# A decoder step with 32 streamed experts: two set-aside blocks of 2 MB that are filled twice, picks by replaced maxima, and sample logits behind the first gather

## The reference, cut to what matters

```python
h = rms_norm(x, norm2_g) * (1.0 + sc2) + sh2
logits = h @ router_w + router_b                 # 264 x 32
top_val, top_idx = lax.top_k(logits, 4)
gate = jax.nn.softmax(top_val, axis=-1)
...
u = xblk @ w_up[e] + b_up[e]                     # 1024 x 2048 per expert, 8 MB
act = glu * jax.nn.sigmoid(1.702 * glu) * (lin + 1.0)
return act @ w_down[e] + b_down[e]               # 1024 x 1024 per expert, 4 MB
```

## Time and profile before

| | before |
|---|---|
| median of 3 runs | 1181.11 us (1179.96 to 1181.35) |
| the profiled execution's own time | 1180.3 us |
| its span, first to last instruction | 1178.5 us |
| PE busy | 1118.9 us, 95% of the span |
| DVE, ACT, POOL busy | 413.6, 191.0, 29.2 us |
| moved by DMA | 460.96 MB, mean 391 GB/s |

### The profile page before, as it was taken

One profiled execution on the slowest core, in us unless ns is written; L12 is line 12 of the kernel. 1 busy time (PEld: TensorE's weight loads), 2 busy tenths in 40 slices (PEclk: granted clock), 3 DMA queues, 4 the chain that ended last, 5 costly groups with the idle time before them and its releaser, 6 DMA issues.

```text
span 1178.5 us, 14278 instructions
## 1 busy us (share of the span) xinstructions
PE 1118.9 (95%) x5652; PEld 499.4 (42%) x5652; DVE 413.6 (35%) x847; ACT 191.0 (16%) x384; POOL 29.2 (2%) x59
## 2 busy tenths in 40 slices
PE   6999998999999999999999989999999999999996
PEld 4777676763333333333333333333333333333332
DVE  3135552352333333333333343333333333333324
ACT  2161222221111111111111111111111111111112
POOL 0201010000000000000000000000000000000001
PEclk8999999999999999999999999999999999999999
DMA  9998994879999999999999999999999999999995
GB/s 348 360 309 220 355 288 156 356 263 408 392 428 429 428 427 428 427 428 429 429 429 429 428 427 427 429 428 426 428 428 427 429 427 428 428 430 427 427 428 207
DMA packets 51178, 460.96 MB, mean 391 GB/s; under 512 B 7012, under 2 KB 7984, under 8 KB 24472
## 3 DMA queue, kind: packets, MB, share of 16 engines
q1 hardware_dynamic: 44864, 449.66, 92.3%
q0 software_dynamic: 2752, 9.47, 3.3%
q10 hardware_dynamic: 3512, 1.14, 0.4%
HBM read 455.60 MB, written 4.65 MB: 391 GB/s over the span
## 4 chain that ended last, share of the span: by engine, by line
PE 64%; DMA 26%; DVE 1%; ACT 1%; issue 0%; ACTq 0%; DVEq 0%; SPq 0%
PE bank L1408 25%; DMA ring<-in_w_up 23%; PE bank L1462 13%; PE bank L1058 5%; PE bank L1449 5%; PE bank L1379 3%; DMA ring<-in_w_down 3%; PE bank L1293 3%; PE bank L1426 2%; PE bank L1022 1%; PE bank L1388 1%; PE bank L1178 1%; PE bank L1437 1%; PE bank L1155 1%; PE bank L1259 1%
## 5 line engine op out<-in xcount | busy, mean ns | idle before, releaser
L1408 PE MATMUL bank<-ring,arena 128*64 128x512 f32 x2032 | 452.6, 595 | 26.4 <-DMA ring<-in_w_up 25.0
L1408 PEld LDWEIGHTS bank<-ring,arena 128*64 128x64 f32 x2032 | 141.4, 137 | 328.1 <-issue 276.9
L1462 PE MATMUL bank<-ring,arena 128*64 128x512 f32 x1024 | 227.2, 595 | 1.6 <-DMA ring<-in_w_down 1.6
L1462 PEld LDWEIGHTS bank<-ring,arena 128*64 128x64 f32 x1024 | 70.8, 137 | 135.7 <-issue 132.8
L1058 PE MATMUL bank<-arena,ring 128*128 128x264 f32 x448 | 109.2, 399 | 2.7 <-DMA ring<-in_w_in 1.9
L1058 PEld LDWEIGHTS bank<-arena,ring 128*128 128x128 f32 x448 | 85.2, 195 | 20.6 <-issue 3.8
L2022 DVE COPY arena<-bank 128x512 f32<-128x512 f32 x32 | 22.1, 691 | 204.2 <-PE bank L1408 204.2
L881 ACT ACTIVATE arena<-bank 128x512 f32<-128x512 f32 x32 | 19.1, 598 | 445.7 <-PE bank L1408 445.7
L2076 DVE TENSOR_TENSOR arena<-bank,arena 128x512 f32<-128x512 f32 x32 | 22.1, 691 | 189.4 <-PE bank L1462 189.4
L1449 PE MATMUL bank<-arena 64*128 64x512 f32 x256 | 80.7, 627 | 0.8 <-issue 0.8
L2071 DVE TENSOR_TENSOR arena<-arena,bank 128x512 f32<-128x512 f32 x128 | 79.1, 680 | 5.4 <-PE bank L1449 5.4
(11 more groups left out here) (327 smaller groups left out, 679.8 us busy)
## 6 DMA issues: line engine op xcount, KB each, us to landing
ring<-in_w_up SPq DMA_DIRECT2D x126, 2048.0 KB, 31.2
ring<-in_w_down SPq DMA_DIRECT2D x63, 2048.0 KB, 29.0
ring<-in_w_ada SPq DMA_DIRECT2D x16, 1024.0 KB, 14.7
ring<-in_w_in SPq DMA_DIRECT2D x14, 1024.0 KB, 15.7
ring<-in_w_ada SPq DMA_DIRECT2D x16, 512.0 KB, 11.3
ring<-in_w_o SPq DMA_DIRECT2D x4, 1024.0 KB, 14.1
ring<-in_state_hgrn POOLq DMA_DIRECT2D x4, 512.0 KB, 14.4
arena<-sample_values POOLq DMA_DIRECT2D x4, 512.0 KB, 14.4
```

What stands on the lines that cost most here:

```text
L1408: last = mm(bank[64 * half:64 * half + 64, b, :], xe[:, par, k % 4, k // 4, :], src[:, 512 * half:512 * half + 512], start=(k == 0), stop= ...
L1462: last = mm(bank[64 * half:64 * half + 64, b, :], acts[:, k, :], pairs[:, slot, D * kk + 512 * half:D * kk + 512 * half + 512], start=(k = ...
```

## The change

Four things change.

**A second set-aside block, and both are filled twice.** A tile `more` of 128 x 3 x 1024 and 1024 columns of `arena` make a second block of 2 MB. Loads 8 and 9 go to the two blocks, and so do loads 18 and 19. Three of the four pieces of load 9 are issued behind the last load of the front, ahead of load 0; the fourth comes after loads 6 and 7, once the prompt's logits are made. The first load into a used ring slot is now load 10 (`FIRST_REFILL`). By the new `load_ahead`, loads 10 to 27 each wait for the load ten before them, and load 28 waits for 20, load 29 for 21, and so on (eight apart), as before the change.

**Picks by replaced maxima.** The logits get four more columns with a huge value, so that the eight maxima are these four and the four best. `match_replace` puts another value in place of all eight, and `picked` is where the logits and the result differ. The gates are computed on all 32 experts and masked by `picked`.

**Order in the routing stretch.** The dummy matmuls go. The count matmuls and the samples' logits and blocks come behind the first gather. All row vectors come behind the first `turn`. The new value of `x` for the prompt is signalled before that for the samples, and ACT squares the samples apart.

**Space.** The constructor's scratch for software-made descriptors is set to 4096 bytes for each partition, where it was left at its default. Some small tiles move or go. The unrolled rounds at the start are 4 instead of 3, and the round with the biases is 16 instead of 15.

```diff
-ASIDE = UPS + UP_FIRST + DOWNS
+ASIDE_AT = UPS + UP_FIRST + DOWNS
+FIRST_REFILL = ASIDE_AT + 2
+ASIDES = (ASIDE_AT, ASIDE_AT + 1, FIRST_REFILL + PAIRS, FIRST_REFILL + PAIRS + 1)
 def ring_place(i):
-    return i - (i > ASIDE)
+    return i - sum(i > a for a in ASIDES)
 def load_ahead(i):
     r = ring_place(i) - PAIRS
-    return r + (r >= ASIDE)
+    return next(j for j in range(r, r + len(ASIDES) + 1) if j not in ASIDES and ring_place(j) == r)
...
+        more = sb("more", [P, 3, 1024])
+        gpickT = sb("gpickT", [P, TP])[:, :]
...
-        aside = [[r_gv[:, 0:1024], r_gv[:, 2112:3136]], [r_qf[:, 2048:3072], r_s[:, 512:1536]]]
+        aside = [[r_gv[:, 0:1024], r_gv[:, 2112:3136], r_qf[:, 2048:3072], r_s[:, 512:1536]],
+                 [more[:, 0, :], more[:, 1, :], more[:, 2, :], r_gv[:, 1024:2048]]]
...
                     if i == UPS + UP_FIRST:
-                        load_aside()
-                    if i == ASIDE:
+                        sp.wait_ge(sem("on_ready"), 4)
+                        sp.wait_ge(sem("S2_out"), 48)
+                        load_aside(ASIDES[0])
+                    if i == ASIDES[0]:
+                        sp.wait_ge(sem("logit_psum"), 1)
+                        load_aside(ASIDES[1], (3,))
+                    if i in ASIDES[:2]:
+                        continue
+                    if i in ASIDES:
+                        name, value = expert_released(ASIDES[ASIDES.index(i) - 2], 0)
+                        sp.wait_ge(sem(name), value)
+                        load_aside(i)
                         continue
                     reuse(i, q)
...
+            load_aside(ASIDES[1], (0, 1, 2))
             for i in range(UPS):
                 reuse(i)
                 load(i, 0, "up", i)
...
-            keep_going(7)
             pe.wait_ge(sem("picked_ready"), 1)
             for i in range(2):
                 for j in range(i + 1):
-                    mm(bank[:, 2, P + NE * i:P + NE * i + NE], before[:, :] if j == i else ones[:, :], picked[:, j, :],
-                       start=(j == 0), stop=(j == i))
-            for j in range(2):
-                last = mm(bank[:, 2, P + 3 * NE:P + 4 * NE], ones[:, :], picked[:, j, :], start=(j == 0), stop=(j == 1))
+                    last = mm(bank[:, 2, P + NE * i:P + NE * i + NE], before[:, :] if j == i else ones[:, :], picked[:, j, :],
+                              start=(j == 0), stop=(j == i))
             last.then_inc(sem("rank_psum"), 1)
...
                 for i in tiles:
-                    od.did(v.max_index(top_i[:, i, :], top_v[:, i, :], logit[:, i, :]))
+                    od.did(v.match_replace(replaced[:, i, :], top_v[:, i, :], logit[:, i, :], -ABOVE))
                 od.settle()
                 own = slice(tiles[0], tiles[-1] + 1)
-                od.link(v.tensor_copy(top_f[:, own, :], top_i[:, own, 0:TOPK]))
-                for i in tiles:
-                    od.did(TT(onehot[:, i], iota_exp[:, :].unsqueeze(1).to_broadcast([P, TOPK, NE]),
-                              top_f[:, i, :].unsqueeze(2).to_broadcast([P, TOPK, NE]), ALU.is_equal))
-                od.settle()
+                od.link(TT(picked[:, own, :], logit[:, own, 0:NE], replaced[:, own, 0:NE], ALU.not_equal), sem("picked_ready"))
...
-    nc = bacc.Bacc("TRN2", target_bir_lowering=False, num_devices=1)
+    nc = bacc.Bacc("TRN2", target_bir_lowering=False, num_devices=1, dynamic_dma_scratch_size=4096)
```

More of the change, by code:

```diff
@@ L19 @@
 I32 = mybir.dt.int32
-U32 = mybir.dt.uint32
 U8 = mybir.dt.uint8
@@ L45 @@
 LIMIT = 7.0
+ABOVE = 3.0e38
 NQ = 6
@@ L841, in _ @@
                 act.wait_ge(sem("x1_ready"), k + 1)
-                od.did(A(tmpT[:, k, :], xT[:, k, :], ACT.Square), sem("sq_ready"))
+                od.did(A(tmpT[:, k, 0:TP], xT[:, k, 0:TP], ACT.Square), sem("sq_ready"))
+                if k == KT - 1:
+                    act.wait_ge(sem("x1s_ready"), KT)
+                    od.did(A(tmpT[:, :, TP:T], xT[:, :, TP:T], ACT.Square), sem("sq_ready"))
                 if k == 0:
@@ L902, in _ @@
             act.wait_ge(sem("gate_sub"), 1)
-            od.did(A(gate[:, :, :], gate[:, :, :], ACT.Exp), sem("gate_exp"))
+            od.did(A(gateE[:, :, :], gateE[:, :, :], ACT.Exp), sem("gate_exp"))
             for i in range(2):
@@ L1356, in _, with samples_routed @@
                 for j in range(i + 1):
-                    mm(bank[:, 2, P + NE * i:P + NE * i + NE], before[:, :] if j == i else ones[:, :], picked[:, j, :],
-                       start=(j == 0), stop=(j == i))
-            for j in range(2):
-                last = mm(bank[:, 2, P + 3 * NE:P + 4 * NE], ones[:, :], picked[:, j, :], start=(j == 0), stop=(j == 1))
+                    last = mm(bank[:, 2, P + NE * i:P + NE * i + NE], before[:, :] if j == i else ones[:, :], picked[:, j, :],
+                              start=(j == 0), stop=(j == i))
             last.then_inc(sem("rank_psum"), 1)
-            pe.wait_ge(sem("h2s_ready"), 1)
-            for k in range(KT):
-                last = mm(bank[0:TS, 3, 0:NE], h2T[:, k, TP:T], wrt[:, k, :], start=(k == 0), stop=(k == KT - 1))
-            last.then_inc(sem("logit_psum"), 1)
-            spread_d(3 * P, TS, lambda g: h2T[:, g:KT:2, TP:T]).then_inc(sem("xs_psum"), 1)
+            def samples_routed():
+                pe.wait_ge(sem("h2s_ready"), 1)
+                spread_d(3 * P, TS, lambda g: h2T[:, g:KT:2, TP:T]).then_inc(sem("xs_psum"), 1)
+                for k in range(KT):
+                    mm(bank[0:TS, 3, 0:NE], h2T[:, k, TP:T], wrt[:, k, :], start=(k == 0), stop=(k == KT - 1))
+                for j in range(2):
+                    last = mm(bank[:, 3, NE:2 * NE], ones[:, :], picked[:, j, :], start=(j == 0), stop=(j == 1))
+                last.then_inc(sem("logit_psum"), 1)
             def gather(n, first_blocks=True):
@@ L1389, in turn, with up @@
                 last.then_inc(sem("turned"), 1)
-            def up(par, k0, k1, loads, rounds, first=False, parts=False):
+            def up(par, k0, k1, loads, rounds, first=False, parts=None):
                 for s in range(k0, k1):
                     slot = loads(s)
-                    if slot is None:
-                        pe.wait_ge(sem("aside_in"), 64)
+                    if slot < 0:
+                        pe.wait_ge(sem("aside_in"), rounds(s))
                     else:
                         pe.wait_ge(sem(f"pair{slot}"), rounds(s))
-                    if parts and s == UPS - 1:
+                    if s == parts:
                         pe.wait_ge(sem("parts_in"), 32)
@@ L1579, in _ @@
             total = LOADS * NE
-            full = [16 * sum(expert_slot(m) == expert_slot(OVER_FIRST + i) for m in range(total) if m != ASIDE) for i in range(LOADS)]
+            full = [16 * sum(expert_slot(m) == expert_slot(OVER_FIRST + i) for m in range(total) if m not in ASIDES) for i in range(LOADS)]
             pe.wait_ge(sem("table_ready"), 1)
```

123 lines of the change are left out of this document (59 added, 64 removed).

## The result

| | before | changed kernel |
|---|---|---|
| median, all runs on this chip | 1179.84 us (1176.37 to 1181.35, 6 runs) | 1171.74 us (1170.14 to 1175.94, 6 runs) |
| the profiled execution's own time | 1180.3 us | 1170.1 us |
| its span | 1178.5 us | 1168.4 us |

The ratio is 0.9936, 95% interval 0.9915 to 0.9957: faster by 5.1 to 10.0 us. The forecast was 1176.6, in a range of 1174.6 to 1178.9.

The account below looks back on a forecast made before the run. DMA was taken as the bound: its last standstill, plus remaining loads at 4.90 us each, plus a fixed tail. Median 1181.1 less 4.5 (ring 4.4, routing 0.1) gave 1176.6 us, range 1174.6 to 1178.9.

Parts of the forecast that it names:

- the base of the sum: Starting figures of the kernel before: span 1178.5 us and median 1181.1, from which 4.4 and 0.1 us of gains were subtracted.
- rival 1: PE, without dummies, drops to half clock around 248 us; costs some 1.7 us, load 30 at 1178.3's pace; chance 0.08.
- The ring: Second filling closes DMA's hole at load 18; load 30 becomes the last dry place, landing at 365.7 not 370.1: 4.4 us gained.
- The pieces: Loads 18 and 19 as eight 512 KB pieces move at 401 GB/s against 430: 0.7 us, hidden, so nothing paid.
- slack: At load 30: the stream could land it at 364.0, PE's release allows 365.7, so 1.7 us of DMA delay costs nothing.
- The second block: Its 2 MB load into DMA holes at 177 and 250 us: no cost, and no gain with only one filling.
- The routing stretch: Picks to first expert matmul: gather starts near 246.2, then 5.6 us of PE work, `up` at 251.8: 0.1 us gained.
- Rival 3: POOL's state transfers wait because the 4096-byte scratch is too small; 1184.6 us if the fourth is 8 us late; chance 0.05.
- the cover: POOL's fourth state could be issued up to 57.7 instead of 43.1 us without delaying ACT: 14.6 us of room.
- Rival 2: Pieces of loads 18 and 19 move nearer to 245 GB/s, load 30 lands at 371.4, time 1182.3 us; chance 0.05.
- Theory B: Posed for the follow-up runs, not in the prediction: the change itself gives the 4.5 us gained ahead of the routing stretch.

Follow-up runs that it names:

- one filling: The changed kernel with both set-aside blocks kept but filled only once (loads 8 and 9): 1177.60 us, ratio 0.9995 to the kernel before.
- one block: The changed kernel with a single set-aside block filled once, as before the change, the rest of the change kept: 1176.92 us, ratio 0.9998 to before.
- the third filling: The changed kernel with the two set-aside blocks filled once more, by loads 28 and 29: 1172.31 us, ratio 0.9951 to the kernel before.

## Why the prediction was wrong, point by point

**The step that failed is the base of the sum.** It took the profiled span of before, 1178.5, and the median of its three runs, 1181.1, and set everything ahead of the routing stretch to no change. That front had been an unlucky one, with a granted clock of 0.61 at 200 to 202 and 0.82 at 206 to 208; a second trace of the same kernel was 3.9 us shorter there, and by the column "clock" 3.4 of them were clock. The medians go the same way. In 68 later runs of the kernel before, the granted clock of each execution is on record: the 19 runs at 0.987 or less have a median of 1180.1 us, the 26 at 0.991 or more one of 1176.7. Over 74 runs in four sessions the medians of before were 1177.8 to 1179.8, so the base was up to 3.3 us too high. The range failed with it: it took 0.7 us as the runs' spread, from three runs, where the 68 go from 1172.4 to 1182.5. With 1177.8 and the 5.1 us of the two terms below, the forecast would have been 1172.7; two of the three medians of the changed kernel are 1172.64 and 1172.72, and the first, on which the result rests, is 1171.74. The result's own pair differs by 8.1 us, the two later ones by 5.1 and 5.2; so some 3 us of the result are chance, 2 of them in the six runs of before (1179.84) and 1 in the six of the changed kernel.

The clock stood in the forecast as a loss only (rival 1, "around 248"). The same rows could have been read the other way: a loss that the trace of before already holds need not come again. Rival 1 came true in one trace in three of the changed kernel, at the price it had been given.

**The ring: right.** Predicted 4.4 us. The four traces with distance eight at load 18 give 820.5 to 820.9 (mean 820.7), the seven with two fillings 814.7 to 817.2 (mean 816.2): 4.5 us. The seven lie 2.5 us apart, and why is open; a single pair of traces would have given 3.3 to 6.2. The hole moved from load 18 to load 30, and one filling or one block gives none of it.

**The pieces: the mechanism right, twice the size.** At 292 to 302 the rate was 369 against 427: (1 - 369/427) x 10 = 1.4 us, not 0.7. The slack held it. What remained was the hole of 0.9 us at 352 to 355 ((1 - 300/427) x 3). The forecast had 1.7 - 0.7 = 1.0 there, which is right by two errors: with 1.4 for the pieces its slack would have left 0.3, so by these estimates the slack was some 0.6 larger than counted. Nor is the price a fixed one: around the pieces of the third filling, at 336 to 352, the rate was 414, which is 0.5 us for two loads.

**The second block: right.** Three pieces went out at 163.3 to 165.7, the fourth at 238.1; filled once it changes nothing.

**The routing stretch: mis-sized.** Predicted 0.1 us, measured 0.68. The gather started where it was expected (246.1 against 246.2 in the times of before). What was missed is behind it: the forecast called PE's 5.6 us from 246.26 to 251.86 free of holes and carried them over. In the kernel before, the sixteen row-vector matmuls stood in two halves around the first `turn`, at these rows of PE's timeline:

```profile
249.38 1.04 PE L1259 MATMUL bank<-ident,modT 128*64 128x128 f32 x8
250.35 0.74 PE L1388 MATMUL bank<-ident,arena 128*128 128x128 f32 x4
251.02 1.09 PE L1259 MATMUL bank<-ident,modT 128*64 128x128 f32 x8
```

From its start to the next row's, the first half took 0.97 us and the second 0.84 (to 251.86), 1.81 together. In the changed kernel all sixteen, with one expert matmul among them, took 246.79 - 245.37 = 1.42. The whole piece from the gather to `up` is 246.79 - 241.63 = 5.16 instead of 5.6. That is 0.44 of the missing 0.58; the rest is spread over the gather's start and the first refill behind `up`. A row of matmuls without a marked idle time isn't proof that each follows at its own pace. One wait is in the rows of PE's weight loads: in the kernel before, ACT's copy of the gathered tokens ended at 250.20, and `turn` began right behind it:

```profile
250.34 0.55 PEld L1388 LDWEIGHTS bank<-ident,arena 128*128 128x128 f32 x4 [0.17 <-ACT arena L869]
```

In the changed kernel the copy ended at 244.20 and `turn` began at 244.73, with no wait. What made the second half as slow wasn't tried.

**Rival 3: its mechanism came true, its price didn't.** POOL stood still for 9.95 us with the small scratch; the fourth state was issued at 48.3, against 57.7 as the latest that costs nothing. The Trainium skill (DMA: Bandwidth & Descriptors, "SWDGE vs HWDGE vs iDMA") has GpSimd write these descriptors into rings in SBUF; the pauses at POOL's issues, which neither trace of before had, agree with a smaller ring. That the cover was counted (14.6 us) kept the chance low, and rightly.

**Rival 2 didn't happen:** 369 GB/s is far from 245.

**Theory B is refuted as far as the runs go:** fronts of the kernel before took 238.2 and 234.3 us, of the changed one 233.7, 235.6 and 235.5; with the clock's loss taken off they are 229.7 and 229.1 against 230.3, 228.8 and 230.3. The kernel with one filling, which has the changed front, had lost as much to the clock as the first trace of before (8.5 us) and needed as long (238.8).

## What to carry to other kernels

A single trace is a sample: before a forecast takes a span as its base, ask which of its stretches at half clock would come again, and give a gain of that kind a chance as well as a loss. When a stream runs dry because a buffer comes free late, find the last dry place, and price an extra buffer by how often it is filled up to there, not by its size. Transfers issued by an engine that computes cost their issue time on its path; look for an idle queue for them.

## What the runs showed of the hardware

**Half-clock stretches and holes of PE.** Seven of 14 traces had a stretch at 1.2 GHz between 196 and 212 us. The hole of PE at the output task, a few us ahead, was 2.40, 2.05, 3.69, 1.92, 1.73, 0.41 and 2.34 us long in these, and 1.96, 2.27, 0, 1.60, 2.11, 0.41 and 0.41 in the seven without (0: PE had no hole, its dummies filled it). So the length of the hole doesn't separate the two groups; the shortest one had a stretch once in three. What decides it in a single execution stays open. What it costs is plain: a front took 228.4 to 231.7 us plus what the clock took, 0 to 8.6 us.

**The issue of a transfer by ACT** took between 0.62 and 2.15 us for the same 64 KB (1.39 to 3.54 us for two), while SP was issuing loads of 2 MB. POOL issued the same two in 1.21 us in each of three traces. That SP's issues are what holds up ACT's was not tried; SP's first load went out at 191.55 us in the trace with 1.39 and at 191.62 in the one with 3.54, so the moment alone doesn't decide it.

**The pauses of POOL.** In the two traces of before POOL issued eight states in 6.5 us without a pause. With the scratch of 4096 bytes the first three went out in 2.86 us, and the fourth 6.4 us later in the first trace of the changed kernel.
